# The memory's norm, two weight pieces and the first GEMM ahead of the small setup work; the bias copies to DRAM in five spaced transfers

## The reference, cut to what matters

```
mem_n = rmsnorm(mem, g_mem)                      # 256 x 1024, one g_mem for each of two layers
kv    = einsum('bmd,dn->bmn', mem_n, w_mem_kv)   # keys and values of the memory attention
h     = rmsnorm(x, g_norm)
z     = einsum('bsd,dn->bsn', h, w_in)           # 13312 columns: q, k, v, gates of three branches
bias  = bias_tab[t5_bucket(kpos - qpos)]         # 20 heads, depends on kpos - qpos alone
s     = q @ k.T * scale + bias                   # 8 "diff" heads and 3 x 4 "dilated" heads
lam   = exp(dot(lp[0], lp[1])) - exp(dot(lp[2], lp[3])) + lam_init
```

## Time and profile before

| what | before |
|---|---|
| median of 3 runs | 2258.4 us (2258.29 to 2258.73) |
| profiled execution, its own time | 2258.98 us |
| its span in the profile | 2257.2 us |
| mean granted clock of TensorE | 0.989 |
| TensorE busy | 2161.0 us (96%) |
| VectorE, ScalarE, GpSimd busy | 1565.2, 1029.4, 186.2 us |
| moved by DMA | 475.60 MB, 211 GB/s over the span |
| the DMA of the bias table, asked for to landed | 46.4 us |

### The profile page before, as it was taken

The page is one execution under the profiler, slowest core; times in us unless marked ns, Lnnn a source line. Parts: engine busy times, 40 slices in busy tenths (PEclk is TensorE's granted clock), DMA queues, the critical chain, the costliest instruction groups (busy, mean ns, idle before and its releaser), DMA issues.

```text
span 2257.2 us, 33992 instructions
## 1 busy us (share of the span) xinstructions
PE 2161.0 (96%) x13827; PEld 1925.4 (85%) x13827; DVE 1565.2 (69%) x2153; ACT 1029.4 (46%) x1698; POOL 186.2 (8%) x202
## 2 busy tenths in 40 slices
PE   6899999999999999989999999999999999999997
PEld 5799888888998888767999787899898899778996
DVE  5477757766777577566898677899745896657444
ACT  5344445544444455455444444433445434464333
POOL 1000001101000011011001001001000001111000
PEclk9999999999999999999999999999999999999999
DMA  8876745566766445623899534699643697525651
GB/s 281 285 227 229 254 156 165 172 224 225 240 232 233 157 160 173 229 98 126 283 342 346 180 119 143 223 350 356 220 145 131 236 353 242 177 85 177 201 188 66
DMA packets 297104, 475.60 MB, mean 211 GB/s; under 512 B 19936, under 2 KB 151466, under 8 KB 296948
## 3 DMA queue, kind: packets, MB, share of 16 engines
q1 hardware_dynamic: 286548, 440.67, 57.5%
q0 software_dynamic: 10400, 32.76, 4.8%
HBM read 465.88 MB, written 7.47 MB: 210 GB/s over the span
## 4 chain that ended last, share of the span: by engine, by line
PE 87%; DVE 6%; DMA 2%; ACT 2%; issue 2%; POOL 1%; SPq 0%; DVEq 0%; POOLq 0%; ACTq 0%
PE G L138 68%; PE A L138 16%; PE G L141 2%; DVE pool L158 1%; DMA raw<-in_w_in 1%; DVE wlo L150 1%; DVE pool L150 1%; ACT pool L144 1%; POOL sm L150 1%; PE A L141 1%; DVE X L150 1%; ACT HTh L144 0%; DVE sm L155 0%; DMA pool<-mod_rows 0%; DMA pool<-in_ada_b 0%
## 5 line engine op out<-in xcount | busy, mean ns | idle before, releaser
L150 DVE TENSOR_TENSOR wlo<-raw,whi 128x1024 fp32r<-128x1024 f32 x640 | 774.2, 1238 | 199.7 <-ACT whi L144 198.2
L144 ACT ACTIVATE whi<-raw 128x1024 fp32r<-128x1024 f32 x640 | 646.3, 1054 | 211.4 <-DMA raw<-in_ffn_w_gu 91.8
L138 PE MATMUL G<-HTh,whi 128*128 128x256 f32 x2336 | 671.9, 288 | 12.0 <-DVE wlo L150 7.0
L138 PE MATMUL G<-HTh,wlo 128*128 128x256 f32 x2336 | 661.6, 283 | 0.0
L138 PE MATMUL G<-HTl,whi 128*128 128x256 f32 x2336 | 661.5, 283 | 0.0
L138 PEld LDWEIGHTS G<-HTh,whi 128*128 128x128 f32 x2336 | 448.4, 192 | 19.6 <-DVE wlo L150 10.8
L138 PEld LDWEIGHTS G<-HTl,whi 128*128 128x128 f32 x2336 | 448.7, 192 | 2.1
L138 PEld LDWEIGHTS G<-HTh,wlo 128*128 128x128 f32 x2336 | 448.3, 192 | 0.0
L144 ACT ACTIVATE pool<-G 128x512 f32<-128x512 f32 (+2 forms) x208 | 115.4, 573 | 537.6 <-PE G L138 504.3
L138 PE MATMUL G<-whi,HTh 128*128 128x512 f32 (+1 forms) x784 | 314.7, 401 | 26.3 <-DVE wlo L150 14.4
L138 PE MATMUL G<-whi,HTl 128*128 128x512 f32 (+1 forms) x784 | 304.6, 389 | 4.5 <-DVE HTl L158 4.1
(11 more groups left out here) (196 smaller groups left out, 2241.1 us busy)
## 6 DMA issues: line engine op xcount, KB each, us to landing
raw<-in_ada_w SPq DMA_DIRECT2D x192, 512.0 KB, 5.9
raw<-in_ffn_w_gu SPq DMA_DIRECT2D x352, 256.0 KB, 4.9
raw<-in_w_in SPq DMA_DIRECT2D x128, 512.0 KB, 4.5
raw<-in_ffn_w_down SPq DMA_DIRECT2D x88, 512.0 KB, 6.6
raw<-in_w_in SPq DMA_DIRECT2D x160, 256.0 KB, 4.8
raw<-in_swa_w_in SPq DMA_DIRECT2D x24, 512.0 KB, 5.3
pool<-mod_rows POOLq DMA_DIRECT2D x24, 512.0 KB, 6.4
raw<-in_gla_w_in SPq DMA_DIRECT2D x24, 512.0 KB, 5.2
```

The lines of the kernel that those rows point to most:

```text
L138: return self.e.matmul(out, a, b, start=start, stop=stop, skip_group_check=True) if self.e else self
L144: return self.e.activation(out, a, func, bias=bias, scale=scale, accum_out=accum) if self.e else self
L150: return self.e.tensor_tensor(out, a, b, op) if self.e else self
```

## The change

The order of the first calls is altered. The memory's load is cut in two halves (`mem0`, `mem1`), so that the squares of the first half wait for it alone. The gain `gm0` is asked for straight after them, the first two pieces of weights come ahead of x, `gm1` and `gn0` (`refill(2)`), and `gm1` moves from GpSimd's queue to SP's. The rest of the setup becomes two closures, `columns` and `table`, called after steps 0 and 1 of the first GEMM; the second layer's rows, the squares of x and the copies of the bias table are handed to `self.soon` as well. The bias table goes to DRAM in five transfers of four heads each (8 to 11, 12 to 15, 16 to 19, 0 to 3, 4 to 7), called at ticks 4, 8, 12, 24 and 32, each waiting for the step that has just been emitted (`self.step`). A reading of a head waits for its own transfer alone.

```diff
@@ gemm
             self.give(n, used)
+            self.step = used
@@ setup
-        self.tmem = self.load("SP", "mem0", memb.a.rearrange("p (t d) -> p t d", t=2),
-                              I["mem"][0].rearrange("(t p) d -> p t d", p=P))
+        self.tmem = [self.load("SP", f"mem{t}", memb.a[:, t * D:t * D + D], I["mem"][0][t * P:t * P + P, :]) for t in range(2)]
+        self.gm = [self.row_gain("gm0", I["g_mem"][0], "SP"), None]
...
-        self.tx = self.load("SP", "x", M.X[:, :, :], I["x"][0].rearrange("(t p) d -> p t d", p=P))
-        self.gm = [self.row_gain("gm0", I["g_mem"][0], "SP"), None]
-        self.gn = self.row_gain("gn0", I["g_norm"][0], "SP")
-        self.gm[1] = self.row_gain("gm1", I["g_mem"][1])
...
+        self.early = 0
+        self.refill(2)
+        self.tx = self.load("SP", "x", M.X[:, :, :], I["x"][0].rearrange("(t p) d -> p t d", p=P))
+        self.gm[1] = self.row_gain("gm1", I["g_mem"][1], "SP")
+        self.gn = self.row_gain("gn0", I["g_norm"][0], "SP")
+
+        def columns():
...
+        def table():
...
+        self.small = [columns, table]
+
+    def write_scratch(self, k):
+
+        h = (8, 12, 16, 0, 4)[k]
+        self.scr[h // 4] = self.load("POOL", f"scr{k}", self.M.scratch[h:h + 4],
+                                     self.btb.a[h:h + 4, :].unsqueeze(1).to_broadcast([4, P, 512]), [self.tbt, self.step])
+        if k == 4:
+            self.btb.release(list(self.scr.values()))
@@ get_bias
-            self.h_bias(r, src, self.scr[0], self.bias_free[r], ev)
+            self.h_bias(r, src, self.scr[h // 4], self.bias_free[r], ev)
@@ mem_kv
+        self.rest()
+        self.early = None
...
+        self.soon += [[1, self.small[0]], [2, self.small[1]], [2, lambda: rows1(0)], [3, lambda: rows1(1)],
+                      [3, lambda: squares(0)], [4, lambda: squares(1)]]
+        self.soon += [[at, lambda k=k: self.write_scratch(k)] for k, at in enumerate((4, 8, 12, 24, 32))]
         self.mkvb = [{"k": self.mk_blk(4)}]
-        used = self.gemm(self.HT, 0, ("mkv", 0, 0), D, "FF", self.ev_copy(self.mkvb[0]["k"]))
-        self.write_scratch(used)
+        self.gemm(self.HT, 0, ("mkv", 0, 0), D, "FF", self.ev_copy(self.mkvb[0]["k"]))
```

More of the change, by code:

```diff
@@ L445, in __init__ @@
         self.acc = None
-        self.modq, self.mod_ev, self.deferred, self.scr = [], {}, [], []
+        self.modq, self.mod_ev, self.deferred, self.scr, self.step = [], {}, [], {}, None
         self.bias_free, self.bias_at = [[] for _ in range(6)], list(range(6))
@@ L1061, in setup @@
             for u in range(2):
-                self.square(N, t, u, memb.a[:, t * D + u * 512:t * D + u * 512 + 512], self.tmem, self.mk_blk(2))
+                self.square(N, t, u, memb.a[:, t * D + u * 512:t * D + u * 512 + 512], self.tmem[t], self.mk_blk(2))
         self.trmem = [self.rstd(*self.mean(t, N), r=M.rmem[:, t:t + 1])[1] for t in range(2)]
-        g, g2 = self.gbank(), self.gbank()
-        trs, self.tcols, self.tadb, self.tc8 = self.new("pe_tr"), self.new("ve_set"), self.new("ve_set"), self.new("ve_set")
@@ new lines, in setup @@
+        self.refill(2)
[3 more added lines that the diff above has]
+        def columns():
+            g, g2 = self.gbank(), self.gbank()
+            trs, self.tcols, self.tadb, self.tc8 = self.new("pe_tr"), self.new("ve_set"), self.new("ve_set"), self.new("ve_set")
+            self.h_cols(g, g2, vr, ab, [tid, tvr] + tab + self.gfree[g] + self.gfree[g2], trs, self.tcols, self.tadb, self.smc(8), self.new("ac_set"), self.tc8)
+            self.gfree[g], self.gfree[g2] = [self.tcols], [self.tadb]
+            vrows.release([trs])
+            for b in ab:
+                b.release([trs])
@@ new lines, in table @@
+        def table():
+            self.tnlam = self.new("ve_set")
+            self.h_lam(lamb, rbb, self.smc(4), tlam, self.new("ve_set"), self.new("ac_set"), self.tnlam)
+            lamb.release([self.tnlam])
+            g = self.gbank()
+            self.btb = self.mk_blk(2)
+            mm, self.tbt = self.new("pe_tr"), self.new("ve_set")
+            self.h_btab(g, rbt, oh, dmk, self.btb, [toh, trb] + self.gfree[g], tdm, mm, self.tbt)
+            self.gfree[g] = [self.tbt]
+            for b in (ohb, rbb):
+                b.release([self.tbt, mm, self.tnlam])
@@ L1266, in fin, with mem_rows @@
                                                  scol=self.M.cols[:, COL["head"]:COL["head"] + 2]))
[L1269 to L1277, removed]
+    def mem_rows(self, t, src, dst, gm, ready):
+        done = [self.new("ve_n"), self.new("ve_n")]
+        for c in range(2):
+            w = slice(t * D + c * 512, t * D + c * 512 + 512)
+            self.h_rows(dst[:, w], src[:, w], self.M.rmem[:, t:t + 1], gm.a[:, c * 512:c * 512 + 512], ALU.mult,
+                        [self.trmem[t]] + ready + gm.tok, done[c])
+        if t:
+            gm.release([done[1]])
         return done
@@ L1282, in mem_kv, with rows1, squares @@
         memb, b0 = self.memb, self.mk_blk(8)
-        d0 = self.mem_rows(memb.a, b0.a, self.gm[0], [self.tmem] + b0.w)
+        d0 = [self.mem_rows(t, memb.a, b0.a, self.gm[0], [self.tmem[t]] + b0.w) for t in range(2)]
         b0.release(self.to_T(lambda t: b0.a[:, t * D:t * D + D], [[[x] for x in d] for d in d0], self.HT))
-        d1 = self.mem_rows(memb.a, memb.a, self.gm[1], [d0[1][1]])
-        N = Norm(self, self.gn)
-        for t in range(2):
+        self.rest()
+        self.early = None
+        N, d1 = Norm(self, self.gn), [None, None]
+        def rows1(t):
+            d1[t] = self.mem_rows(t, memb.a, memb.a, self.gm[1], [d0[t][1]])
+        def squares(t):
             for u in range(2):
@@ L1338, in layer1 @@
         gemm(HT, 0, ("mq", l), D, "FF", self.ev_copy(B["q"]))
-        if l == 0:
-            self.btb.release(self.scr)
         gemm(HT, 0, ("mg", l), D, "FF", self.ev_silu(B["g"]))
@@ L1957, in run @@
         assert self.piece == len(self.stream) and not self.halves
-        self.h_end(stored, self.scr[0])
+        self.h_end(stored, list(self.scr.values()))
 class Apart:
@@ L3251, in h_end @@
     def h_end(self, stored, scr):
-        for t in stored + [scr]:
+        for t in stored + scr:
             self.e.wait_ge(*self.at(t))
```

## The result

The changed kernel takes **2331.8 us** (median of 4 runs, 2328.7 to 2335.0) against 2258.5 of the kernel before (2258.29 to 2258.73). The ratio is 1.0325, 95% interval 1.0313 to 1.0338. So it is slower, as forecast, but by 73 us and not by 33, and outside the range. The profiled execution took 2328.7.

What follows compares the result with a forecast made beforehand. TensorE bounds the kernel, apart from its late first GEMM and waits behind the bias table's DMA. 2257.2 - 6.4 + 1.3 - 13.9 + 46.5 + 5 = 2289.7, plus 1.2 gives 2291 us; range 2236 to 2316.

Steps and rivals of the forecast that it cites:

- The mechanism of a transfer: Each bias table transfer reads one group of four partitions on four engines, other engines each time, taking 41 us.
- short transfers: Rival for the five bias table transfers: each takes 9 us, by bytes, no step waits; 2240 us, chance 0.24.
- four engines, no shared group: Rival for the five bias table transfers: 64 packets at 0.32 us, 20 us each; 2246 us, chance 0.12.
- always the same four engines: Rival for the five bias table transfers: they queue behind each other on fixed engines; 2391 us, chance 0.18.
- The one transfer goes, -13.9: Removing the old bias table transfer wins 13.9 us: TensorE's four waits and the lower clock behind them.
- The start, -6.4: At the beginning, TensorE's first GEMM starts at 18.0 instead of 24.38, winning 6.4 us.
- The 1.3 for columns and table: Columns and table move from the idle beginning to between first GEMM steps, costing TensorE 1.3 us (bounds 1 and 3).
- the sum of the waits, +46.5: Waits of TensorE for weight pieces held up by the five bias table transfers cost 46.5 us.
- The first transfer: Moving from 36 to 77, it makes step 15 wait 12 us for its weight piece.
- The second to the fourth: Second: step 17 waits 6.5 us; third: none; fourth: pieces of steps 29 and 30 are 3 and 14.5 late.
- The fifth: Asked for after step 27, moving 126 to 167: pieces of steps 34 and 35 are 5.5 and 5 us late.
- The clock, +5: After the three longest waits TensorE runs at the lower clock, 1.4 to 1.9 us each, 5 us.

Runs made afterwards that it cites:

- stride5: The changed kernel with only the choice of heads altered: transfer k takes heads k, k+5, k+10, k+15 instead of four neighbouring ones; 2248.2 us, ratio 0.9954.
- dram_before: The kernel before, with only the bias table's way to DRAM altered: stored once, then copied from DRAM to DRAM over 16 engines; 2244.8 us, ratio 0.9935.
- start_only: The kernel before with the new order of the first calls, the bias table still in one transfer of 20 heads, called at tick 4; 2256.95 us, ratio 0.9985.
- dram_copy: The changed kernel with the table stored once and copied 128 times from DRAM to DRAM over 16 engines, replacing the five transfers; 2241.9 us, ratio 0.9926.
- late_block: The changed kernel with the bias table's block given back 40 ticks after the fifth transfer is called; 2331.3 us, ratio 1.0309.
- more32: `dram_copy` plus one needless transfer of heads 4 to 7 to an unread place in DRAM, at tick 32; 2270.2 us, ratio 1.0045.
- stride4: The changed kernel with four transfers of five heads (k, k+4, ..., k+16), one from each group of four partitions, at ticks 4, 8, 12, 24; 2242.9 us, ratio 0.9924.
- ident_first: `stride4` with the identity asked for before the memory's halves; 2241.1 us, ratio 0.9921.

## Why the prediction was right or wrong, point by point

- **The mechanism of a transfer was right.** Four engines for each transfer, one shared source group (0.61 us a packet; 41 to 45 us to landing forecast, 43.8 to 49.4 measured), other engines for each transfer, one weight packet to one bias packet. `stride5` shows that the choice of rows does it, so the rivals "short transfers" and "four engines, no shared group" fall for this kernel; the latter's 2246 is near what `stride5` gives once the groups differ (2248). Landing times of 49.4 at most, where it had 80 and 120, rule out "always the same four engines".
- **The one transfer goes, -13.9: right.** `dram_before`, where the copy over 16 engines replaces it, is 14.2 us under its kernel before.
- **The start, -6.4: too large.** It was -3.9. I put the identity's delay at 1.7 with an upper bound of 2.3; it was 4.3. `start_only` gives 3.4 for the start as a whole (0.15%), and `dram_copy` against `dram_before` 2.9 by the times, with intervals that overlap; -3.9 + 1.3 is 2.6. The 1.3 for columns and table was right: on TensorE they stand between steps from 24.98 to 25.20 and from 28.24 to 29.20, 1.2 in all.
- **The step that failed: the sum of the waits, +46.5.** It was 78.1, and it failed in three places.
  - *The first transfer*, 18.9 (18.58 and 0.27) where I had 12. I let TensorE run on until step 15. It stopped before step 12, because the copy that it needed stands on ScalarE behind the split of step 14's late piece. Step 15's piece was usable at 84.1, where I had 79.5. An estimate from these rows: without that order TensorE would have gone on at 61.6, waited 12.2 for step 14 and 1.9 for step 15, so 14.1.
  - *The second to the fourth*, 28.4 where I had 24.0. That this is near is luck. I had put 17.5 of it at steps 29 and 30, where TensorE waited for nothing; it waited 15.5 before steps 16 to 18 and 12.9 before steps 20 to 22. The fourth was asked for at 94.65 and not at 103.5, since it waited for step 15 and not for the head; what that alone cost, no run shows.
  - *The fifth*, "5.5 and 5 late", 10.5 in all, which measured 30.8. `late_block` shows the part of the weights: step 34 was not late at all, and step 35 was 19.6. TensorE was not short of work, it went on for 28.8 us after the transfer was asked for (as in `more32`). But the piece of step 35 landed only when the transfer was over, and I had let it pass earlier. Which pieces ahead of it filled its place was not traced. One such transfer costs 27 us or more at any of three places.
- **What I had not seen:** the reuse of the table's block as a wait of VectorE. It is in the trace, but worth only 4 to 5 us beside the late weights, which is too little for the times to show clearly.
- **The clock, +5: about half of what it was.** I had counted three waits, and there were more. A step of 24 matmuls takes 2.83 us from its first to its last start at the full clock (47.75 to 50.58), but 4.33 and 5.07 behind the waits that end at 130.34 and 141.47; the granted clock was 0.55 from 136 to 147. An estimate from TensorE's rows behind all its waits is 10 us. With the measured terms the sum is 2257.2 - 3.9 + 1.3 - 13.9 + 78.1 = 2318.8, and the span is 2326.9: 8.1 are left for the lower clock and for the rest.

## What to carry to other kernels

Here a broadcast of 1.05 MB out of four neighbouring partitions moved 27 GB/s, and on its four engines it held up every other DMA that needed a share of them. Cutting such a transfer into parts helps only if each part reads from different groups. Dealt by stride, the same bytes left TensorE one wait, of 1.3 us (`stride4`) or 4.4 us (`stride5`); copied from DRAM to DRAM over all engines, none of as long as 1 us.

Before pricing a late load, ask what else stands behind it on an engine that works in order: a step can wait for a late piece that it does not use. Check on which event a transfer really waits. And do not trust that the wait named last is the only one: take it away and look for the second behind it.

## What the runs showed of the hardware that I had not expected

- Three loads ahead of the identity on one queue move its landing from 2.0 us after asking (`ident_first`, 0.74 to 2.70) to 7.7 (`stride4`, 2.13 to 9.87), although they hold only 1.5 MB.
- Asking itself slows down: with one slow transfer in flight SP took 11.20 us to ask for the two halves of one piece (`more32`), where it takes 0.88 in `dram_copy`.
- A copy from DRAM to DRAM of 5.24 MB beside the weights reached 363 GB/s in all (`dram_copy`, 44 to 60 us) and left TensorE no wait of as long as 1 us.
